# The normed input at two places of its buffer: offset 0 in the feed-forward stages, 704 bytes up in mixer, attention and mLSTM

## What is computed

```python
h = x
mod = silu(c) @ w_ada + b_ada                       # 9 vectors: shift, scale, gate, three times
u = rmsnorm(h) * (1 + sc1) + sh1
h = h + 0.5 * g1 * (silu(u @ up_a) * (u @ up_b)) @ down      # feed-forward 1, width 2816
u = rmsnorm(h) * (1 + sc2) + sh2
h = h + g2 * hybrid_mixer(u)        # projections of u, gated delta rule both ways, gates, w_out
u = rmsnorm(h) * (1 + sc3) + sh3
h = h + 0.5 * g3 * swiglu(u)                        # feed-forward 2
h = rmsnorm(h)
h = h + diff_attention(rmsnorm(h))                  # q, k, v from one projection
h = h + relu(rmsnorm(h) @ w1[0])**2 @ w2[0]         # width 4096
h = h + mlstm_mixer(rmsnorm(h))
h = h + relu(rmsnorm(h) @ w1[1])**2 @ w2[1]
return rmsnorm(h)
```

## The kernel before, in words

| buffer | address in a partition, before | residue in 1 KB |
|---|---|---|
| `w_hi0`..`3`, `w_lo0`..`3` | 49152 to 81920, 4 KB each | 0 (second m tile 512) |
| `u_hl` | 90112 | 0 |
| `a_hl0` | 106496 | 0 |
| `a_hl1`, `mid_hl` | 133824 | 704 |
| `mg_hl` | 191424 | 960 |

## Time and profile before

### The profile page before, as it was taken

One profiled execution on the slowest core, in us unless ns is written; L12 is line 12 of the kernel. 1 busy time (PEld: TensorE's weight loads), 2 busy tenths in 40 slices (PEclk: granted clock), 3 DMA queues, 4 the chain that ended last, 5 costly groups with the idle time before them and its releaser, 6 DMA issues.

```text
span 1377.3 us, 26212 instructions
## 1 busy us (share of the span) xinstructions
PE 1333.5 (97%) x10705; PEld 1191.4 (87%) x10705; DVE 918.7 (67%) x1403; ACT 708.7 (51%) x1156; POOL 740.5 (54%) x821
## 2 busy tenths in 40 slices
PE   6999999999999998999999999999999999999997
PEld 2888887898989888888888999988999899988886
DVE  4788797797998477766445677686544775766432
ACT  2655533774555334465554557655544555555442
POOL 0777673442333324746655584376756443766653
PEclk9999999999999999999999999999999999999999
DMA  9888977644335434657546644456555444656551
GB/s 364 282 276 271 342 266 230 199 155 124 109 119 174 154 102 135 202 188 241 196 153 227 226 150 152 129 170 194 185 196 185 152 140 136 194 162 195 199 193 52
DMA packets 226301, 258.98 MB, mean 188 GB/s; under 512 B 8505, under 2 KB 195335, under 8 KB 226055
## 3 DMA queue, kind: packets, MB, share of 16 engines
q1 hardware_dynamic: 221968, 252.74, 56.1%
q10 hardware_dynamic: 4215, 4.58, 1.0%
HBM read 256.24 MB, written 2.63 MB: 188 GB/s over the span
## 4 chain that ended last, share of the span: by engine, by line
PE 82%; DVE 11%; ACT 3%; issue 2%; DMA 1%; POOL 0%; SPq 0%; ACTq 0%; DVEq 0%
PE ps L755 26%; PE ps L749 25%; PE ps L751 12%; PE ps L775 6%; PE ps L794 3%; DVE w_lo L2058 2%; DMA raw<-in_w_ada 1%; DVE mt L2330 1%; ACT w_hi L1438 1%; DVE sil L2330 1%; PE ps L1111 1%; PE ps L711 1%; PE ps L1100 1%; PE ps L840 1%; PE ps L1154 1%
## 5 line engine op out<-in xcount | busy, mean ns | idle before, releaser
L683 POOL TENSOR_TENSOR w_lo<-raw,w_hi 128x256 fp32r<-128x256 f32 x800 | 725.3, 937 | 621.2 <-ACT w_hi L1438 621.2
L1438 ACT CAST w_hi<-raw 128x1024 fp32r<-128x1024 f32 (+1 forms) x408 | 412.4, 1044 | 174.8 <-PE ps L755 61.7
L749 PE MATMUL ps<-u_hl,w_hi 128*128 128x512 f32 x1216 | 428.2, 397 | 4.5 <-DVE u_hl L2143 2.8
L2058 DVE TENSOR_TENSOR w_lo<-raw,w_hi 128x1024 fp32r<-128x1024 f32 x204 | 274.7, 1347 | 112.8 <-ACT w_hi L1438 111.0
L751 PE MATMUL ps<-u_hl,w_lo 128*128 128x256 f32 x1216 | 338.6, 278 | 0.0
L755 PE MATMUL ps<-u_hl,w_hi 128*128 128x256 f32 x1600 | 298.0, 287 | 2.9 <-DVE yaf L2310 1.4
L749 PEld LDWEIGHTS ps<-u_hl,w_hi 128*128 128x128 f32 x1216 | 228.1, 188 | 63.6 <-issue 7.1
L755 PEld LDWEIGHTS ps<-u_hl,w_hi 128*128 128x128 f32 x1600 | 248.5, 191 | 12.8 <-issue 8.0
L751 PEld LDWEIGHTS ps<-u_hl,w_lo 128*128 128x128 f32 x1216 | 228.9, 188 | 0.1
L755 PE MATMUL ps<-u_hl,w_lo 128*128 128x256 f32 x800 | 226.1, 283 | 0.0
L755 PEld LDWEIGHTS ps<-u_hl,w_lo 128*128 128x128 f32 x800 | 153.1, 191 | 0.0
(11 more groups left out here) (395 smaller groups left out, 1836.6 us busy)
## 6 DMA issues: line engine op xcount, KB each, us to landing
raw<-in_mlp_w SPq DMA_DIRECT2D x64, 1024.0 KB, 5.3
raw<-in_w_ffn_up SPq DMA_DIRECT2D x44, 1024.0 KB, 5.1
raw<-in_w_ada SPq DMA_DIRECT2D x30, 1024.0 KB, 5.8
raw<-in_w_in SPq DMA_DIRECT2D x30, 1024.0 KB, 5.7
raw<-in_w_ffn_down SPq DMA_DIRECT2D x16, 1024.0 KB, 5.9
raw<-in_attn_w_in SPq DMA_DIRECT2D x12, 1024.0 KB, 4.9
raw<-in_mlstm_w_in SPq DMA_DIRECT2D x12, 1024.0 KB, 5.2
aside<-in_w_ada SPq DMA_DIRECT2D x6, 1024.0 KB, 8.4
```

The source lines that it names most:

```text
L683: pool.tensor_tensor(w_lo[half][:, kt, :], src[:, kt, :], w_hi[half][:, kt, :].bitcast(F32), ALU.subtract).then_inc(low_ready(n, h)[0], 1)
L749: pe.matmul(two(b - 10 + m), x, z, start=(first and kt == ks.start), stop=False, skip_group_check=True)
L1438: act.copy(w_hi[t % HALVES][:, 0:k, :], src).then_inc(hi_ready, 1)
L2058: dve.tensor_tensor(w_lo[half][:, 0:k, :], src, w_hi[half][:, 0:k, :].bitcast(F32), sub)\
```

## The change

A table `U_AT` names for each stage at which of two offsets the normed input lies: 0 in the four feed-forward stages, 704 bytes in mixer, attention and mLSTM. Two tensors over the same memory, 704 bytes apart, take the place of `u_hl`, and each reader and writer takes the one of its stage. `a_hl0` moves up by 704 bytes. To make room, all buffers behind them (`uf`, `x_tm`, `cst`, the small ones, `mid_hl`, `a_hl1`, `mg_hl` and what else lies above) move up by exactly 1 KB, so that their residues in 1 KB stay. `raw`, `w_hi`, `w_lo` and `hT` stay where they are. Apart from addresses, every engine has the same instructions with the same shapes and the same waits in the same order as before; nothing is added, removed or moved in time by the program.

```diff
+U_AT = {"ffn1": 0, "mix": 704, "ffn2": 0, "attn": 704, "mlp0": 0, "mlstm": 704, "mlp1": 0}
...
-        u_hl = at("u_hl", [P, KD, 2, S], F32R, 72 * KB)
-        u_hi, u_lo = u_hl[:, :, 0, :], u_hl[:, :, 1, :]
-        uf = at("uf", [P, KD, S], F32, 88 * KB)
-        x_tm = at("x_tm", [P, 2, D], F32, 88 * KB)
+        u_set = {x: at(f"u_hl{x}", [P, KD, 2, S], F32R, 72 * KB + x) for x in sorted(set(U_AT.values()))}
+        uf = at("uf", [P, KD, S], F32, 89 * KB)
+        x_tm = at("x_tm", [P, 2, D], F32, 89 * KB)
         C_np, C_at = constants()
-        cst = at("cst", [P, C_np.shape[1]], F32, 96 * KB)
-        o = 96 * KB + 4 * C_np.shape[1]
+        cst = at("cst", [P, C_np.shape[1]], F32, 97 * KB)
+        o = 97 * KB + 4 * C_np.shape[1]
...
-        a_hl = [at("a_hl0", [P, 4, 2, S], F32R, 88 * KB), at("a_hl1", [P, 4, 2, S], F32R, big)]
+        a_hl = [at("a_hl0", [P, 4, 2, S], F32R, 88 * KB + 704), at("a_hl1", [P, 4, 2, S], F32R, big)]
...
+        def u_parts(name):
+
+            u = u_set[U_AT[name]]
+            return u[:, :, 0, :], u[:, :, 1, :]
...
-                    hi, lo = (u_hl[:, kt, c, t * P:(t + 1) * P] for c in range(2))
+                    hi, lo = (u[:, kt, c, t * P:(t + 1) * P] for c in range(2))
...
-            U, MIDS = (lambda k: u_hl[:, k]), (lambda k: mid_hl[:, :, k])
+            U, MIDS = (lambda name: lambda k: u_set[U_AT[name]][:, k]), (lambda k: mid_hl[:, :, k])
...
-                            half(plan.slab[(kind, key)], h, b, U, h == 0, h == 1, first)
+                            half(plan.slab[(kind, key)], h, b, U("mix"), h == 0, h == 1, first)
...
-                columns("wb", 4, U, (s("yb_ready"), 0, 4))
+                columns("wb", 4, U("mix"), (s("yb_ready"), 0, 4))
```

More of the change, by code:

```diff
@@ L434, in build @@
         t1 = at("t1", [P, HG, P], F32, dl + 38 * KB)
-        zs = [at("zs0", [P, HG, S], F32, dl + 40 * KB), at("zs1", [P, HG, S], F32, 92 * KB)]
-        attm = at("attm", [P, 4, HG, CH], F32, 88 * KB)
+        zs = [at("zs0", [P, HG, S], F32, dl + 40 * KB), at("zs1", [P, HG, S], F32, 93 * KB)]
+        attm = at("attm", [P, 4, HG, CH], F32, 89 * KB)
         tok = at("tok", [P, 12, 32], F32, dl + 44 * KB)
@@ L779, in tok_half, with by_tokens @@
                 mm.then_inc(halves_done, 1)
-            def by_tokens(n, h, b):
+            def by_tokens(n, h, b, u):
                 i = (2 * n + h) % HALVES
@@ L822, in first_slab @@
                 between = {1: lambda: ada_sums(1, (1,)), 3: lambda: mod_sums(1)}
-                half(n, 0, b, U, True, False, ready, between)
+                half(n, 0, b, U("ffn1"), True, False, ready, between)
                 warm(1)
-                half(n, 1, b, U, False, True, ready)
+                half(n, 1, b, U("ffn1"), False, True, ready)
             def warm(n):
@@ L855, in ffn @@
                         else:
-                            slab((name, i, t), (name, i, t), U, ready=ready if i == 0 else None)
+                            slab((name, i, t), (name, i, t), U(norm), ready=ready if i == 0 else None)
                     if i - 2 in ups:
@@ L887, in mlp @@
             def mlp(name, norm, then):
-                columns(name, 16, U, u_ready(norm), due=norm)
+                columns(name, 16, U(norm), u_ready(norm), due=norm)
                 for g in range(4):
@@ L902, in last_mlp @@
                 for j in range(16):
-                    slab(("m1", j), ("m1", j), U, ready=u_ready("mlp1") if j == 0 else None)
+                    slab(("m1", j), ("m1", j), U("mlp1"), ready=u_ready("mlp1") if j == 0 else None)
                     if j == 1:
@@ L1284, in attention @@
                         if j < 8:
-                            half(plan.slab[("aqkv", j)], h, b, U, h == 0, h == 1, u_ready("attn") if i == 0 else None)
+                            half(plan.slab[("aqkv", j)], h, b, U("attn"), h == 0, h == 1, u_ready("attn") if i == 0 else None)
                         else:
-                            by_tokens(plan.slab[("aqkv", j)], h, b)
+                            by_tokens(plan.slab[("aqkv", j)], h, b, u_set[U_AT["attn"]])
                         after(2 * i + h)
@@ L1407, in mlstm @@
                         if key[0] == "mvo" and key[1] < ML_H:
-                            by_tokens(plan.slab[key], h, b)
+                            by_tokens(plan.slab[key], h, b, u_set[U_AT["mlstm"]])
                         else:
-                            half(plan.slab[key], h, b, U, h == 0, h == 1, u_ready("mlstm") if i == 0 else None)
+                            half(plan.slab[key], h, b, U("mlstm"), h == 0, h == 1, u_ready("mlstm") if i == 0 else None)
                         after(2 * i + h)
@@ L1491, in shifted @@
                     act.wait_ge(s("uf_ready"), first + k + 1)
-                    act.activation(u_hi[:, k, :], uf[:, k, :], ACT.Identity, bias=mod_at(shift)[:, k:k + 1])\
+                    act.activation(u_parts(name)[0][:, k, :], uf[:, k, :], ACT.Identity, bias=mod_at(shift)[:, k:k + 1])\
                         .then_inc(s("u_hi_ready"), 1)
@@ L1500, in fresh @@
                 for k in (2 * c, 2 * c + 1):
-                    op = act.activation(u_hi[:, k, :], hT[:, k, :], ACT.Copy, scale=g[:, k:k + 1])
+                    op = act.activation(u_parts(name)[0][:, k, :], hT[:, k, :], ACT.Copy, scale=g[:, k:k + 1])
                 op.then_inc(s("u_hi_ready"), 2)
@@ L1726, in heads_hi @@
             def heads_hi(c):
-                act.copy(u_hi[:, 4 * c:4 * c + 4, :], qkv[:, 4 * c:4 * c + 4, :]).then_inc(s("yb_hi_ready"), 1)
+                act.copy(u_parts("mix")[0][:, 4 * c:4 * c + 4, :], qkv[:, 4 * c:4 * c + 4, :]).then_inc(s("yb_hi_ready"), 1)
             def delta(hh, fill):
@@ L2134, in low @@
                 for k in (2 * c, 2 * c + 1):
-                    op = dve.scalar_tensor_tensor(u_lo[:, k, :], hT[:, k, :], g[:, k:k + 1], u_hi[:, k, :].bitcast(F32), mul, sub)
+                    op = dve.scalar_tensor_tensor(u_parts(name)[1][:, k, :], hT[:, k, :], g[:, k:k + 1],
+                                                  u_parts(name)[0][:, k, :].bitcast(F32), mul, sub)
                 op.then_inc(s("u_ready"), 2)
@@ L2142, in shifted_low @@
                 dve.wait_ge(s("u_hi_ready"), 8 * SPLIT.index(name) + k + 1)
-                dve.scalar_tensor_tensor(u_lo[:, k, :], uf[:, k, :], mod_at(MODS[name])[:, k:k + 1],
-                                         u_hi[:, k, :].bitcast(F32), add, sub).then_inc(s("u_ready"), 1)
+                dve.scalar_tensor_tensor(u_parts(name)[1][:, k, :], uf[:, k, :], mod_at(MODS[name])[:, k:k + 1],
+                                         u_parts(name)[0][:, k, :].bitcast(F32), add, sub).then_inc(s("u_ready"), 1)
             def norm(name):
@@ L2502, in heads_low @@
                 sl = slice(4 * c, 4 * c + 4)
-                dve.tensor_tensor(u_lo[:, sl, :], qkv[:, sl, :], u_hi[:, sl, :].bitcast(F32), sub)\
+                dve.tensor_tensor(u_parts("mix")[1][:, sl, :], qkv[:, sl, :], u_parts("mix")[0][:, sl, :].bitcast(F32), sub)\
                     .then_inc(s("yb_ready"), 1)
```

## The result

The changed kernel takes 1373.67 us (median of 6 runs, 1371.38 to 1376.89), beside 1380.43 us for the kernel before in the same rounds (6 runs, 1378.23 to 1382.91). The ratio is 0.995, with an interval of 0.9936 to 0.9964: about 6.9 us are won (5.0 to 8.8), where 13.0 were forecast. The time lies 8.1 us above the 1365.6 us of the prediction. The profiled executions differ by 5.9 us (1378.96 and 1373.09).

What follows compares the result with a forecast made beforehand. TensorE's matmul pace was taken as the bound (busy 1333.5 of 1377.3 us). Gains of 11.4 + 0.6 + 1.0 = 13.0 us from 1378.6 us gave 1365.6 us, range 1360 to 1375 us.

Steps and rivals of the forecast that it cites:

- the first step: L755 on `u_hl`: residue 704 instead of 0 brings matmul starts to 113 to 114 ns apart, `wb` to 21.8 us.
- the region: Rival: whether buffers lie above or below address 131072 sets the pace, so the time stays 1378.6 us; chance 0.13.
- the forecast's own case: Whole kernel: 10 to 17 us won, 1361.6 to 1368.6 us; chance 0.64.
- the case that everything is kept: Rival: the gain counts also where VectorE is on the chain, L794 in full; 18.7 us won, 1359.9 us; chance 0.06.
- the first term of the sum: L755 on `u_hl` in mixer, `wb`, attention and mLSTM: 5.4% of 211.5 us on the chain, 11.4 us won.
- L794's 1.0: L794 in attention and mLSTM, `u_hl` stationary: 1.0 us won, the middle between 0 and 1.9 us.
- Part 1: L755 on `u_hl`, 2400 matmuls: 6.5 ns of 119.8 less each, counted where on the chain, 11.4 us won.
- part 5: Feed-forward up projections, L749 and L751: two cadences, no change taken; ends 2.7 us won or 5.5 us lost.
- put down to its layout and gave 0.08: Rival: `u_hl` gets only the pace of `mid_hl`, 1.8% less; 4.1 us won, 1374.5 us; chance 0.08.
- Part 2: `a_hl0` in attention's output projection: 96 matmuls from 120 to 113.3 ns, 0.6 us won.
- Part 3: L794, 384 matmuls with `u_hl` stationary: between 0 and 5.4% of 35.3 us on the chain, taken as 1.0 us.
- Part 4: Other buffers moved 1 KB: costs nothing, since `mid_hl` gets addresses it already has and stays at 117.6 ns.

## Why the prediction was right in sign and nearly twice too large

The sign, the place and the mechanism of the first step were right. `wb` came to 21.69 us (21.8 forecast), the region was refuted, L749 and L751 kept their cadences on the whole, and the shift cost nothing (0.9994). The time, 1373.67 us, lies between the forecast's own case and no change, in the range but only because the range took in other cases. (The range's lower end, 1360 us, leaves out the case that everything is kept, 1359.9, by 0.1 us, which the text doesn't count among what it leaves out.) The text named this outcome: `wb` at 21.8 us and less than 10 us won means an error in what lies on the chain or in the cadences. It was both: the first term of the sum, 11.4 us, priced every matmul at the faster of two cadences, and counted the gain in full wherever L755 was on the chain before. With L794's 1.0 it stood for 12.4 us; mixer, `wb`, attention and mLSTM gave 7.0 (3.4 + 1.3 + 0.6 + 1.7).

**Part 1, the pace: 6.5 ns of 119.8, taken for every matmul.** The rows behind it were one buffer in one place, `a_hl1`, and `wb`'s estimate from it. At distance 192 the stream has two cadences, and outside `wb` the mean is 114.7 to 114.9 ns, 5.1 ns less instead of 6.5. On the 188.5 us of chain other than `wb` (211.5 - 22.95) that is 8.0 us instead of 10.2. The warning stood in my own text: part 5 allowed two cadences for the pair, and the earlier trace rows had `mid_hl` at 117.6 ns at the same residue, which I put down to its layout and gave 0.08. It was a second cadence, not a second kind of buffer: the version with three matmuls has `mid_hl` at 113.3 ns in m0.

**Part 1, the chain: 211.5 us of L755, all of whose gain counts.** The chain that ended last tells what was critical, not by how much. Attention was forecast at 46.5 us x 5.4% = 2.5 us, and with its share of L794 (20.5 us x 2.7%) 3.1. It kept 0.6, since the softmax lay less than 2 us behind, and 2.1 once that was lighter (0.5 of the difference was pace). The mixer was forecast at 5.8 us; at the measured pace 106.8 x 5.1 / 119.8 = 4.5 were left, and 3.4 were kept, 5.3 with lighter convolutions. The text named VectorE there and wrote that the sum already leaves out what it holds back. That was the error: the share on the chain before leaves out what VectorE held back at the old pace, not what it holds back at the new one. The mLSTM gave 1.7 (1.9 from L755 and 0.4 from L794 forecast, 1.9 in all at the measured paces). There too TensorE was busy for 2.5 us less and idle for 0.7 us more, 2.1 instead of 1.4, but the chain had left most of that out.

**Part 2,** `a_hl0`: 114.5 ns, 0.5 us of pace instead of 0.6, of which the stage kept 0.2. **Part 3,** L794: the middle that I took, 2.7%, is close in pace (116.1 of 119.6, 2.9%), for a reason that I didn't have: its distance is 64, not 192, and it mixes 113 and 118 ns there. In attention at most the 0.6 us, which is for both lines, was kept. **Part 4** was right for the time, and wrong in its reason: `mid_hl` doesn't keep its pace because its addresses are alike, it can run at 113.3 or at 117.8 ns at one and the same addresses. **Part 5** was right at zero, within what varies: a pair takes 349.2, 348.3, 352.3 and 347.1 ns in the four up projections, where it took 347.4, 348.1, 351.9 and 349.0.

The Trainium skill, "SBUF — State Buffer", section "Who interferes with whom", has the two read ports of TensorE independent. By that rule the time would have stayed; the windows of `wb` say otherwise, by 6.5 ns in 119.5, and so do those of the stream by itself, by 6.7 ns in 120, with nothing but addresses different and no other engine at work.

In numbers, the forecast of 13.0 us goes to 10.9 by the measured paces (8.0 + 1.3 + 0.5 + 35.3 us x 3% = 1.1). Of that the stages kept 7.2 in the profile: 7.0 as above and 0.2 on `a_hl0`. What was given back is 2.0 us in attention, 1.1 in the mixer and some 0.2 in the mLSTM, to work on VectorE and ScalarE, and 0.3 behind `a_hl0`. The rest of the profiled 5.9 us was in no part of the sum: 1.4 us won in `wo`, the mLSTM's output and the last up projection, 1.1 lost in the first up projection and 1.6 to the clock. That the median gain, 6.9 us, comes close to the 7.2 is luck in part.

## What to carry to other kernels

- Where matmuls with a load each stream back to back, look at the distance of their starts by buffer, and try the moving operand 192 bytes above the stationary one modulo 256: here that was worth 5.6% of the stream in its faster cadence and 1.8% in its slower one (113.3 or 117.8 ns instead of 120.0). Check each shape by itself; the pair of 512 and 256 columns took 353.3 ns at that offset after every entry tried, and 346.7 or 353.3 at distance 0.
- A gain of a few per cent on a chain is priced against the chain behind it. Lighten the second engine's work in both kernels, and compare the pair: here 0.6 us became 2.1 and 3.4 became 5.3.
- Before a difference between two profiles is given to the change, or called noise, look at the granted clock of the stretch: here 1.6 us of one profile were a mean of 0.92 instead of 1.00.
- A pace read in one place may be one of several steady cadences. Before it becomes a price, read it in all places with the same addresses; a place with another pace is a warning and not an exception.

## What the runs showed of the hardware that was not expected

The distance of the operands' addresses modulo 256 bytes bears on the pace of 256-column float32r matmuls with one weight load each: with the weights stationary it was 120.0, 117.8, 118.6 and 113.3 ns at 0, 64, 128 and 192 (120.0 at 96; 116.7 at 32, and 117.8 after small matmuls). At 192 the stream holds one of two cadences, 113.3 or 117.8 ns, through all 48 matmuls of a part and, in m0, all 768 of a stage; one matmul more or less of another length ahead of it changed which. With the activation stationary distance 64 has these two cadences too.

The Trainium skill, "TensorE: Matmul & The Clock Gate", section "Back-to-back issue gap", gives 262 cycles for 256 columns, at 2.4 GHz an estimate of 109.2 ns; it calls this the gap of an isolated matmul, and says that in a stream with weight loads both set the spacing. No row here reaches 109.2 ns; the fastest is 113.3 ns, with a weight load for every matmul.

What stays open: why the address matters (no run looks below the operands), what in the way in picks the cadence (the matmuls directly ahead decide it within one kernel of streams, but not between two), which of the mixer's half slabs is entered in which way, and why the clock fell before `wb` in one profile of the changed kernel and not in the other. An offset of 64 for the stages of L794, which the stream by itself favours, wasn't tried in the kernel.
